# Gate-up loop of a decoder step: when VectorE makes each weight block's low part

## The reference

```
def swiglu(h, w_gu, w_down):
    g, u = jnp.split(h @ w_gu, 2, axis=-1)
    return (jax.nn.silu(g) * u) @ w_down
```

## Time and profile before

| | |
|---|---|
| median of 3 runs (lowest to highest) | 933.33 us (933.22 to 936.35) |
| profiled execution, its own time | 940.86 us |
| its span, first to last instruction | 939.1 us |
| granted TensorE clock, mean | 0.99 |

### The profile page before, as it was taken

One profiled execution on the slowest core, in us unless ns is written; L12 is line 12 of the kernel. 1 busy time (PEld: TensorE's weight loads), 2 busy tenths in 40 slices (PEclk: granted clock), 3 DMA queues, 4 the chain that ended last, 5 costly groups with the idle time before them and its releaser, 6 DMA issues.

```text
span 939.1 us, 16499 instructions
## 1 busy us (share of the span) xinstructions
PE 910.1 (97%) x6285; PEld 769.7 (82%) x6285; DVE 637.4 (68%) x1251; ACT 413.6 (44%) x823; POOL 281.0 (30%) x277
## 2 busy tenths in 40 slices
PE   6999999999999999999999998999999999999998
PEld 5777888899996666866775498999999999888886
DVE  3546585488837676768472799899889898443544
ACT  3655562142135343666840574444444446333221
POOL 4110100000015442444600217776777774000000
PEclk9989999999999999999999999999999999999999
DMA  8998603235248987196103163333333333522201
GB/s 266 386 362 272 199 27 114 90 119 222 89 139 309 335 322 266 57 303 173 36 1 112 68 180 85 96 90 91 91 95 103 108 101 109 194 90 90 73 0 51
DMA packets 84188, 138.83 MB, mean 148 GB/s; under 512 B 4180, under 2 KB 54948, under 8 KB 79759
## 3 DMA queue, kind: packets, MB, share of 16 engines
q1 hardware_dynamic: 74578, 96.26, 32.1%
q0 software_dynamic: 9248, 41.39, 12.5%
q10 hardware_dynamic: 284, 0.13, 0.1%
HBM read 130.58 MB, written 11.31 MB: 151 GB/s over the span
## 4 chain that ended last, share of the span: by engine, by line
PE 86%; DVE 6%; DMA 4%; ACT 2%; issue 2%; POOL 1%; SPq 0%; DVEq 0%; ACTq 0%
PE bank L2389 18%; PE bank L2391 18%; PE bank L2390 18%; PE bank L2383 9%; PE bank L2469 3%; PE bank L2910 3%; DMA wring<-in_w_ada 2%; PE bank L2750 2%; PE bank L2418 2%; PE bank L2720 2%; PE bank L2929 2%; PE bank L2883 2%; PE bank L2398 2%; PE bank L2399 2%; PE bank L2674 1%
## 5 line engine op out<-in xcount | busy, mean ns | idle before, releaser
L2389 PE MATMUL bank<-s,ring_hi 128*128 128x288 f32 x620 | 184.6, 298 | 2.7 <-DVE ring_lo L528 2.7
L2390 PE MATMUL bank<-s,ring_lo 128*128 128x288 f32 x620 | 183.6, 296 | 0.0
L2391 PE MATMUL bank<-s,ring_hi 128*128 128x288 f32 x620 | 183.0, 295 | 0.0
L2389 PEld LDWEIGHTS bank<-s,ring_hi 128*128 128x128 f32 x620 | 116.8, 188 | 3.2 <-DVE ring_lo L528 3.1
L2391 PEld LDWEIGHTS bank<-s,ring_hi 128*128 128x128 f32 x620 | 117.4, 189 | 0.0
L2390 PEld LDWEIGHTS bank<-s,ring_lo 128*128 128x128 f32 x620 | 117.1, 189 | 0.0
L528 DVE TENSOR_TENSOR ring_lo<-mem,ring_hi 128x512 fp32r<-128x512 f32 x84 | 108.3, 1325 | 0.8 <-POOL mem L980 0.5
L2383 PEld LDWEIGHTS bank<-cst,arena 128*128 128x128 f32 (+1 forms) x538 | 62.3, 148 | 21.0 <-issue 12.3
L2383 PE MATMUL bank<-cst,arena 128*128 128x128 f32 (+1 forms) x538 | 72.1, 288 | 7.5 <-DMA arena<-in_cache_k_cmp,idx 6.6
L528 DVE TENSOR_TENSOR dn_w<-wring,dn_w 128x2048 fp32r<-128x2048 f32 (+1 forms) x11 | 23.1, 2096 | 65.9 <-ACT dn_w L525 65.9
L900 POOL DMA_INDIRECT arena<-in_cache_k_slc,idh x16 | 15.4, 963 | 172.9 <-PE bank L2391 167.3
(11 more groups left out here) (385 smaller groups left out, 2112.9 us busy)
## 6 DMA issues: line engine op xcount, KB each, us to landing
wring<-in_w_gu SPq DMA_DIRECT2D x44, 512.0 KB, 5.3
wring<-in_w_ada SPq DMA_DIRECT2D x16, 1024.0 KB, 11.0
wring<-in_w_in SPq DMA_DIRECT2D x10, 1024.0 KB, 5.1
wring<-in_w_down SPq DMA_DIRECT2D x10, 1024.0 KB, 5.0
wring<-in_w_ada SPq DMA_DIRECT2D x16, 512.0 KB, 5.8
proj<-in_x_prompt SPq DMA_DIRECT2D x4, 512.0 KB, 11.9
mem<-in_state_k_win POOLq DMA_DIRECT2D x8, 256.0 KB
mem<-in_state_v_win POOLq DMA_DIRECT2D x8, 256.0 KB
```

What stands on the lines that cost most here:

```text
L2389: pe.matmul(dst, sh, ml, start=first and k == 0, stop=False)
L2390: pe.matmul(dst, sl, mh, start=False, stop=False)
L2391: ins = pe.matmul(dst, sh, mh, start=False, stop=last and k == len(pairs) - 1)
```

## The change

In VectorE's loop every step p now makes the low part of slot p + 8, the slot that ScalarE casts in its own step p, one call a step. Before, a step made that of slot p + 7, none in the step after an m = 3, and two in the step of an m = 3. For this one more low part, slot 14, is made ahead of the loop, and the call behind the loop is gone. Nothing else is changed: the instructions are the same, in number and size, and those of ScalarE and SyncE stand in the same order.

```
             slot_rest(13)
+            slot_rest(14)
             for p, (f, m) in enumerate(FAST):
...
-                if p == 7 or FAST[p - 1][1] != 3:
-                    slot_rest(p + 7)
+                slot_rest(p + 8)
                 if p == 8:
                     first_result(3)
                 if m == 3:
-                    if p + 1 < NFAST:
-                        slot_rest(p + 8)
                     want_emptied(dve, key)
...
-            slot_rest(NSLOT + 3)
```

## The result

The changed kernel takes 950.77 us (median of 4 runs, 949.48 to 952.61) against 933.93 us (4 runs, 933.22 to 936.35): ratio 1.0187, 95% interval 1.0167 to 1.0207, or some 17 us slower. The forecast was 933.4, with 929.2 to 936.5 as its range. No change worth naming was forecast, and the time lies far outside.

The account below looks back on a forecast made before the run. TensorE, busy 910.1 of 939.1 us, was taken to bound the kernel. Loop start +0.05, regular rounds 0 and SyncE's loads 0 gave +0.05 us, carried over to 933.33 and rounded to 933.4; range 929.2 to 936.5.

Parts of the forecast that it names:

- What bounds the kernel: Whole kernel: TensorE is busy 910.1 of 939.1 us; only its standstills or lower clock can be won back.
- The start of the loop: Rows from 567 to 587 us: the long TensorE wait stays; +0.05 us, bounds -4.1 and +1.4.
- GpSimd gets the turn at 575.5: Rival, loop start: L972 beats low part (2,7), new 0.8 us wait; 933.5, or 932.1 or 934.9 by clock; chance 0.12.
- my choice: Loop start: VectorE gets its turn for low part (2,7) first, ending at 576.15, ahead of TensorE's need at 576.56.
- its case of 932.1: Loop start, GpSimd first: the last wait shortens to 1.9 us and leaves the clock up; rival's chance 0.12.
- The regular rounds: The 18 regular rounds: TensorE gains nothing, having had no wait there; 0 us, bounds 0 and +5.8.
- the round still closes in 11.20 us: Regular rounds: although the eviction of (10,6) comes at 668.0 instead of 667.85, the round stays 11.20 us.
- I count 0: Regular rounds: the change in time was put at 0 us, with bounds of 0 and +5.8.
- the least left: Regular rounds: the smallest time between a low part's end and TensorE's need is 2.5 us instead of 1.1.
- a wait in each round: Rival, regular rounds: a low part held twice makes TensorE wait once a round; 18 x 0.32 = 5.8 us, 939.1; chance 0.11.
- if TensorE waits in the rounds behind 600: Sign, regular rounds: TensorE waits behind 600 us would show the prediction wrong; it expected 11.20 us a round.
- the 1.4 us: Loop start, behind the 2.45 us wait near 580: 13 matmuls at the lower 1.2 GHz clock cost some 1.4 us more.

Follow-up runs that it names:

- e2: Kernel before, keeping the old order up to product (3,3) and taking the new order from f = 4 on; ratio to before 1.0155.
- e5: Kernel before, keeping the old order up to product (7,3) and taking the new order from f = 8 on; ratio to before 1.0110.
- e12: Kernel before with only the low part of (f,3) moved ahead of the eviction of (f,6); 937.52 us, ratio to before 1.0045.
- e10: Kernel before without the matmul of the weights' high part by the activations' low part from f = 4 on; ratio to before 1.0025.

## Why the prediction was wrong

**What bounds the kernel:** right. TensorE did, and all to be won was small.

**The start of the loop:** one turn was wrong, and the time stayed inside the bounds of that part. Priced at +0.05 us, it gave -1.34. The low part of (2,6) came as in the replay, with a wait of 0.23 us. Then the rival "GpSimd gets the turn at 575.5" came true instead of my choice: a new wait of 0.62 us where that rival has 0.8, and a last one of 1.65 where it has 1.9, with the clock up, its case of 932.1. The exclusive lock of the Trainium skill, page "SBUF — State Buffer", had pointed to it, and this trace agrees with that rule: L972 started first there (569.14 against 569.17) and VectorE's low part took 1.82 us. The gain itself is that of the clock, which in e2 stayed up behind the old wait too: that it came is luck, not the worth of the new order.

**The regular rounds:** here it failed, at the step "the round still closes in 11.20 us". I replayed one round from the places that the engines had before and took it as closed. The mechanism was in my hands: the text says that VectorE now waits for a sum ahead of (10,6) and a cast ahead of (10,3). What I didn't do is add up the waits as a ring, from L980 to L980, and set the sum against 11.20. The replay even had the number: it puts the eviction of (10,6) at 668.0 instead of 667.85, so 0.15 us late, and `t_sum` and the next L980 follow that eviction. 11.20 + 0.15 = 11.35 is the ring, and e5 measured 11.34 with the multiplications free. I took the 0.15 us for nothing. It looks like rounding in a replay of one round; it is decisive in 17 or 18, since the slack that hides it runs out. So the term "I count 0" for the rounds should have been some 18 us. The replay also put the low part of (10,7) ahead of L972 by 0.4 us. In e5 that held for one round only; in the next, L972 was first and held it 1.1 us.

The second thing missed is that the state isn't stable: what I called the least left, 2.5 us, was slack of the low parts against TensorE, but what decides is 0.8 us, by which the second multiplication passes ahead of L972 in the replay (664.05 less 0.45 against 664.38). In e5 it was 0.25 us, then 0.12, then -0.05 (668.54 against 668.59). Once it is gone, further operations are held, the round takes 12.24, and 0.9 us more go.

**The rival "a wait in each round"** came true, at 0.11. Its mechanism was half right: VectorE stands still for a sum and a cast. It looked for a low part that misses two turns; instead the evictions behind the waiting low parts held up ScalarE and GpSimd, who made the next low part late. Its price of 0.32 us a round was the shortest wait in the trace; measured are 1.04. The new bound of a loop can't be priced by a wait that occurs elsewhere.

**The profile's signs:** the text named "if TensorE waits in the rounds behind 600" as what would prove it wrong, and that is what the list of waits shows.

## What to carry to other kernels

An operation moved ahead in an in-order stream takes its wait along to all that stood before it. Where the engines feed one another, follow the releases around once and add them from an operation to the same operation a round later: if the sum is over the bound engine's round, even by 1%, the slack that a replay of one round shows will be gone some rounds on. An earlier result is worth nothing where nobody waited for it; here the low parts had 1.1 us in hand, and the change bought more by tying three engines into a ring.

## What the runs showed of the hardware

A VectorE operation with both inputs in SBUF and a GpSimd one exclude each other in whole instructions, so the time that a round takes has steps. Which of the two is issued some hundredths of a microsecond earlier makes 1.1 us for the one that comes second: the second multiplication took 0.45 us at 657.23, 0.12 us ahead of L972, and 1.56 at 668.59, 0.05 us behind it. The Trainium skill, page "SBUF — State Buffer", section on the two separate sides, states the rule as an exclusive lock, and every hold in these traces agrees; that one order has two lengths of a round by it is what the runs add (11.34 and 12.24 us).

The same wait of TensorE did not have the same sequel. Five traces have the old start with its wait of 2.43 to 2.46 us: behind it the granted clock is 0.66 in before, e5 and e12, and 1.00 in e2 and e10. Here e2 and e5. Their stretches of 5 us from the end of the wait (2.44 and 2.46 us), e2 first; the clock is the third last number:

```profile
573.70:578.70 5.00, 4.94 (x37) 4.94 (x38) 5.00 (x8) 2.39 (x6) 4.49 (x4) 1.00 0.76 213
```

```profile
575.40:580.40 5.00, 4.97 (x26) 4.97 (x27) 4.89 (x8) 0.95 (x2) 2.97 (x3) 0.66 0.78 212
```

In e2 TensorE went on at 2.4 GHz with 37 matmuls in 5 us, in e5 it fell to 1.2 GHz for part of it and did 26, as before did. So the 1.4 us that I put down as a cost of that wait is one of two outcomes of it. What decides between them no run here shows.
